# Re-ordering the state-space stage of a single-core decoder kernel: a chunk copy, two index computations, a lag table and the queue of projection units

## The reference, cut to what matters

```
z = h @ w_in            # q | 6 K/V tiles | branch gates | u (512 S5 channels) | merge gates
bu = einsum('gnc,btgc->btgn', b_bar, u)            # 32 groups, 64 complex states, 16 channels
h_t = a_bar * h_{t-1} + bu_t                       # scan over 512 tokens
y = Re(einsum('gcn,btgn->btgc', c, h)) + d * u     # then gelu, GLU, merge
```

## Time and profile before

| | |
|---|---|
| executions | 1350.45, 1352.05, 1352.19 us |
| the profiled execution | 1350.45 us, its span 1348.7 us |
| busy: PE, DVE, POOL, ACT | 1240.4, 832.8, 360.3, 306.0 us |
| mean granted PE clock | 0.967 of full |
| PE's share of the chain that ended last | 84% |

### The profile page before, as it was taken

One profiled execution on the slowest core, in us unless ns is written; L12 is line 12 of the kernel. 1 busy time (PEld: TensorE's weight loads), 2 busy tenths in 40 slices (PEclk: granted clock), 3 DMA queues, 4 the chain that ended last, 5 costly groups with the idle time before them and its releaser, 6 DMA issues.

```text
span 1348.7 us, 20585 instructions
## 1 busy us (share of the span) xinstructions
PE 1240.4 (92%) x7765; PEld 1007.8 (75%) x7765; DVE 832.8 (62%) x1370; ACT 306.0 (23%) x832; POOL 360.3 (27%) x422
## 2 busy tenths in 40 slices
PE   6889898999998679999999999977999999999995
PEld 5778776678886456555788888766888888888885
DVE  7997332237887468777755655657565464466445
ACT  3465111120010356556211001132000000000012
POOL 5953233322220013222111211110111112513441
PEclk9989998989999889999999999997999999999998
DMA  9324455567667224434653231420131131131101
GB/s 263 92 64 133 153 131 153 150 214 252 242 245 248 71 79 123 157 99 146 234 171 91 81 111 63 168 99 16 63 125 63 63 125 63 63 125 63 63 1 64
DMA packets 122002, 166.15 MB, mean 123 GB/s; under 512 B 36448, under 2 KB 90400, under 8 KB 117552
## 3 DMA queue, kind: packets, MB, share of 16 engines
q1 hardware_dynamic: 103408, 104.72, 25.0%
q0 software_dynamic: 8080, 50.58, 10.6%
q10 hardware_dynamic: 10416, 9.54, 2.2%
HBM read 159.34 MB, written 13.84 MB: 128 GB/s over the span
## 4 chain that ended last, share of the span: by engine, by line
PE 84%; DVE 9%; ACT 3%; issue 3%; POOL 0%; DMA 0%; another core or an unknown queue 0%; DVEq 0%; ACTq 0%; PEldq 0%
PE PS L2287 45%; PE PS L1874 14%; PE PS L2051 9%; PE PS L1851 4%; PE PS L2006 2%; PE PS L2195 2%; PE PS L2163 2%; DVE small L1663 2%; PE PS L2225 1%; DVE PS L1661 1%; DVE R L1681 1%; ACT QO L977 1%; PE PS L2030 1%; PE PS L1989 1%; DVE hT L1263 1%
## 5 line engine op out<-in xcount | busy, mean ns | idle before, releaser
L1874 PE MATMUL PS<-hT,stream 128*128 128x260 f32 (+1 forms) x800 | 186.0, 393 | 1.8 <-DVE hT L1263 0.7
L1874 PEld LDWEIGHTS PS<-hT,stream 128*128 128x128 f32 (+1 forms) x800 | 152.4, 193 | 33.4 <-issue 5.6
L2287 PE MATMUL PS<-R,stream 128*128 128x260 f32 x720 | 168.9, 383 | 2.4 <-PE PS L2287 2.4
L2287 PEld LDWEIGHTS PS<-R,stream 128*128 128x128 f32 x720 | 135.7, 190 | 25.8 <-issue 5.5
L2287 PE MATMUL PS<-R 128*128 128x260 f32 x576 | 134.4, 390 | 3.3 <-DVE R L1826 2.1
L2287 PEld LDWEIGHTS PS<-R 128*128 128x128 f32 x576 | 111.8, 194 | 22.1 <-DVE R L1826 2.5
L2051 PE MATMUL PS<-R 128*128 128x256 f32 (+1 forms) x544 | 121.2, 382 | 5.2 <-DVE R L1504 2.4
L2287 PE MATMUL PS<-R,QO 128*128 128x260 f32 x544 | 123.6, 383 | 1.4 <-DVE QO L1707 1.4
L1781 DVE TENSOR_TENSOR R<-PS,R 128x260 f32<-128x260 f32 x100 | 42.7, 427 | 129.6 <-PE PS L2287 128.9
L2051 PEld LDWEIGHTS PS<-R 128*128 128x128 f32 x544 | 101.4, 195 | 22.1 <-issue 6.1
L2287 PEld LDWEIGHTS PS<-R,QO 128*128 128x128 f32 x544 | 103.3, 190 | 17.6 <-DVE QO L1707 1.8
(11 more groups left out here) (421 smaller groups left out, 1929.2 us busy)
## 6 DMA issues: line engine op xcount, KB each, us to landing
stream<-in_cache_kv_slc SPq DMA_DIRECT2D x128, 128.0 KB, 2.1
stream<-in_w_mlp_up SPq DMA_DIRECT2D x8, 2048.0 KB, 8.3
stream<-in_w_mlp_down SPq DMA_DIRECT2D x8, 2048.0 KB, 7.7
stream<-in_w_in SPq DMA_DIRECT2D x4, 2048.0 KB, 9.4
stream<-in_state_kv_win SPq DMA_DIRECT2D x16, 512.0 KB, 5.6
stream<-in_w_in SPq DMA_DIRECT2D x8, 1024.0 KB, 7.8
out_kv_win_sample<-in_state_kv_win POOLq DMA_DIRECT2D x1, 8176.0 KB, 43.6
R<-in_cache_kv_slc SPq DMA_DIRECT2D x56, 128.0 KB
```

Source lines behind the costliest of these rows:

```text
L1874: ins = M(pair(u)[0:w, hf, 0:HALF], lhs[k], rhs[k][:, HALF * hf:HALF * hf + HALF], start=(k == 0), stop=(k == n - 1))
L2287: ins = M(product_of(w, i), lhs[:, k, :], rhs[:, k, :], start=(k == 0), stop=(k == nk - 1))
```

## The change

It does the following:

- the unit `kt` goes; `kk` makes the table in its final orientation, with `FP` as the stationary operand (128x128) and `C0P` as the moving one (32 columns), into full-width PSUM; `KPS` lives elsewhere;
- `u 3` stands ahead of the last two `ft` units, `y 0..3` one query tile later each (`y 3` behind `q 3`), and chunk ends 1 behind `q 4` where it was behind `q 7`;
- chunk copy 0 goes from ACT to DVE, ahead of the table; the page indices go ahead of the table too;
- chunk copy 1 stands behind the last `ft`, copies 2 and 3 behind `h0`, ahead of `toeplitz`;
- the S5 loop's fourth scratch buffer lies elsewhere, and DVE waits ahead of the loop for `toe_ready` and `gp_ready` (before, for `gp_ready` at ii == 1 and for no `toe_ready`).

```diff
-    head += [("ft", 0, q) for q in range(2)] + [("kt",)] + [("ft", 1, q) for q in range(2)] + u_tiles[3:]
+    head += [("ft", 0, q) for q in range(2)] + u_tiles[3:] + [("ft", 1, q) for q in range(2)]
-    rest = [q_units[6], ("h0",), q_units[7], q_units[4], ("y", 0), q_units[5], ("y", 1), q_units[0], ("y", 2),
-            q_units[1], ("y", 3), q_units[2], q_units[3], ("st",)]
+    rest = [q_units[6], ("h0",), q_units[7], q_units[4], q_units[5], ("y", 0), q_units[0], ("y", 1), q_units[1],
+            ("y", 2), q_units[2], q_units[3], ("y", 3), ("st",)]
-ENDS_BEHIND = [("h0",), ("q", 7), ("y", 0), ("y", 1)]
-COPIES_BEHIND = {("u", 3): 0, ("q", 6): 1, ("q", 7): 2, ("q", 4): 3}
+ENDS_BEHIND = [("h0",), ("q", 4), ("y", 0), ("y", 1)]
+COPIES_BEHIND = {("ft", 1, 1): (1,), ("h0",): (2, 3)}
-        KTS = QO[:, 6464:6976]
-        KPS = KVU[:, 1552:2064].rearrange("p (i c) -> p i c", i=NST)
+        KPS = QO[:, 6464:6976].rearrange("p (i c) -> p i c", i=NST)
-        W5 = [R[:, 14848:14848 + T]] + [QO[:, c:c + T] for c in (6464, 6976, 3 * NT)]
+        W5 = [R[:, 14848:14848 + T]] + [QO[:, c:c + T] for c in (6464, 6976, 7488)]
             elif k == 1:
                 eng.wait_ge(gp_ready, 1)
                 eng.wait_ge(pair_full, U_H0 + 1)
-                eng.wait_ge(toe_ready, 1)
...
-            dve.wait_ge(pair_free, U_KT + 1)
+            dve.wait_ge(pair_free, U_KK + 1)
             link(V.tensor_tensor(KPS[96:128], KPS[96:128], DI[96:128], ALU.add))
             dve.sem_inc(lag_ready, 1)
+            dve.wait_ge(pages_in, 16)
+            dve.wait_ge(masks_in, 16)
+            V.tensor_scalar(row_kv[:, :], pages[:, :], 2.0 * PAGE, consts[:, CO_ROW:CO_ROW + 1], ALU.mult, ALU.add)
...
+            V.tensor_scalar(row_cmp[:, :], pgr, 1.0, consts[:, CO_ROW + 1:CO_ROW + 2],
+                            ALU.mult, ALU.add).then_inc(rows_ready, 1)
+            dve.wait_ge(zero_ready, 3)
+            dve.wait_ge(pair_free, AT["u", 3] + 1)
+            for tau in range(TAU):
+                V.tensor_copy(UC[32 * tau:32 * tau + 32, 0::4, NB:NB + NK], uT[0:32, :, tau:T:TAU])
+            V.tensor_copy(UC[0:32, 0::4, 0:NB], uT[0:32, :, T:NT])
+            V.tensor_copy(UC[96:128, 0::4, NB + NK:UCW], uT[0:32, :, T:NT]).then_inc(chunk0_ready, 1)
             dve.wait_ge(pair_full, U_FT + 1)
             V.tensor_copy(TAB[:, 0, :, 0:64], BAS[:, 0])
...
             dve.wait_ge(pair_free, U_H0 + 1)
+            dve.wait_ge(toe_ready, 1)
+            dve.wait_ge(gp_ready, 1)
...
                 elif kind == "kk":
-                    for q in range(4):
+                    for i in range(NST):
                         for r in range(2):
-                            for i4 in range(4):
-                                i = 4 * q + i4
-                                ins = M(pr[32 * i4:32 * i4 + 32, 0, P * q:P * q + P], C0P[:, r, i, :], FP[:, r, i, :],
-                                        start=(r == 0), stop=(r == 1))
+                            ins = M(pr[:, 0, 32 * i:32 * i + 32], FP[:, r, i, :], C0P[:, r, i, :],
+                                    start=(r == 0), stop=(r == 1))
```

More of the change, by code:

```diff
@@ L302, in build @@
         chunks_ready = sem("chunks_ready")
+        chunk0_ready = sem("chunk0_ready")
         ends_full = sem("ends_full")
@@ L971, in chunk_copies @@
             def chunk_copies(ii):
-                act.wait_ge(pair_free, AT["u", 3] + 1)
+                act.wait_ge(pair_free, UNITS.index(("gemm", ("win", (C_U, 512)), 3, P, ("u", 3))) + 1)
                 act.wait_ge(zero_ready, 3)
@@ L1054, in _ @@
                 elif kind == "kk":
-                    ins = nc.scalar.activation(KTS, pr[:, 0, :], ACT.Copy)
-                elif kind == "kt":
                     ins = nc.scalar.activation(KPS, pr[:, 0, :].rearrange("p (i c) -> p i c", i=NST), ACT.Copy)
@@ L1083, in _ @@
                 ins.then_inc(pair_free, 1)
-                if label(unit) in COPIES_BEHIND:
-                    chunk_copies(COPIES_BEHIND[label(unit)])
+                for ii in COPIES_BEHIND.get(unit, ()):
+                    chunk_copies(ii)
                 if unit == ("h0",):
@@ L1367, in _ @@
                        (NST, m))
-            dve.wait_ge(pair_free, U_KT + 1)
+            dve.wait_ge(pair_free, U_KK + 1)
             link(V.tensor_tensor(KPS[96:128], KPS[96:128], DI[96:128], ALU.add))
             dve.sem_inc(lag_ready, 1)
+            dve.wait_ge(pages_in, 16)
+            dve.wait_ge(masks_in, 16)
+            V.tensor_scalar(row_kv[:, :], pages[:, :], 2.0 * PAGE, consts[:, CO_ROW:CO_ROW + 1], ALU.mult, ALU.add)
+            link(V.tensor_copy(pgf, pages[:, :]))
+            link(V.tensor_tensor(pgf.rearrange("p (x n) -> p x n", n=4), pgf.rearrange("p (x n) -> p x n", n=4),
+                                 consts[:, CO_PG:CO_PG + 4].unsqueeze(1).to_broadcast([P, 4 * NB, 4]), ALU.mult))
+            link(V.tensor_reduce(pgr, pgf.rearrange("p (x n) -> p x n", n=4), AX, ALU.add))
+            V.tensor_scalar(row_cmp[:, :], pgr, 1.0, consts[:, CO_ROW + 1:CO_ROW + 2],
[6 more added lines that the diff above has]
+            V.tensor_copy(UC[96:128, 0::4, NB + NK:UCW], uT[0:32, :, T:NT]).then_inc(chunk0_ready, 1)
             dve.wait_ge(pair_full, U_FT + 1)
@@ L1381, in _ @@
             dve.sem_inc(tables_done, 1)
[L1382 to L1390, removed]
             def sample_states():
-                w4 = [w[:, 0:P].rearrange("p (b i) -> p b i", b=NB) for w in W5[0:3] + [DEC]]
+                w4 = [w[:, 0:P].rearrange("p (b i) -> p b i", b=NB) for w in W5]
                 AR, AI, NI = (x.unsqueeze(1).to_broadcast([P, NB, NST]) for x in (abr, abi, nabi))
@@ L1984, in chunk_ends @@
                     pe.wait_ge(ends_free, ii)
-                pe.wait_ge(chunks_ready, ii + 1)
+                if ii == 0:
+                    pe.wait_ge(chunk0_ready, 1)
+                else:
+                    pe.wait_ge(chunks_ready, ii)
                 for r in range(2):
```

7 lines of the change are left out of this document (removed).

## The result

| | before | changed |
|---|---|---|
| median of 6 runs beside each other | 1352.8 us (1350.45 to 1355.72) | 1361.2 us (1356.15 to 1364.18) |
| ratio | | 1.006, 95% from 1.0036 to 1.0085 |
| profiled execution | 1350.45 us, span 1348.7 | 1360.14 us, span 1358.3 |
| granted clock, mean | 0.967 | 0.964 |

The change makes the kernel 8.4 us slower. Forecast were +5 and slower; 1361.2 lies inside the range (1352.8 to 1362.0) near its upper end, 4.2 us above the forecast of 1357. By the time alone it would fit the rival of the returning stand (1360.5) better; the traces have to decide. Later, on another chip where before takes 1327.6 us, the same change costs 1.0111 (1.0092 to 1.0129), 14.7 us.

The account below looks back on a forecast made before the run. PE was taken as the bound, standing still ahead of chunk ends 0 (for DVE's tables) and st; +5.1 (tables) and +0.2 (pauses) made +5.3, 1355.8 us profiled, 1357 typical, 8-in-10 range 1352.8 to 1362.

Parts of the forecast that it names:

- the rival of the returning stand: PE ahead of y 3: the 3.5 us wait for its own pair_full returns on top, 1360.5; 0.22 with like losses.
- The tables, on DVE: Index instructions (1.9) and copies (3.2) ahead of the tables delay them and chunk ends 0 by 5.1 us (3.9 to 7.1).
- kk and kt, on PE: kk takes 8.0 us instead of 1.95, kt's 0.9 goes; hidden by cover at u 3 and the tables, cost 0.
- theory A: Posed after the profile: the chain kk, ft, u 3 on PE sets when the tables come.
- B: The prediction's theory: the instructions added on DVE ahead of the tables delay them.
- The loop's new wait: DVE waits for ACT's toeplitz from 78.5 to 87.3; each y stands a tile later with 7.6 us over, cost 0.
- y 3 and the K/V tile: kv 0 0 waits for y 3's Gelus, some 4 us, against the lost 3.52 us stand ahead of st; +0.2 net.
- The odd stand: PE's 3.52 us idle ahead of st, waiting for its own pair_full, released by something the profile cannot name.
- Little remains: Rival: fast copies and a partly covered last Gelu, or tables and clock giving back, leave +2 to +2.7, 1354.3; 0.15.
- faster: Rival at the key scores: the shift breaks up pauses of 10 us together, giving 1347; 0.08.
- The tail by DVE's loop: Rival: DVE's loop is the limit, late toe_ready makes y 0 wait, 1361 or more; in the slower tail, no separate chance.

Follow-up runs that it names:

- the old order: The changed kernel with the order of q and y tiles as before, chunk ends 1 behind q 7; 1.011 (1.0074 to 1.0146) against before.
- the early copies: The kernel before with five small DVE instructions that begin BAS, two 128x16 copies among them, moved some 1.4 us earlier; 0.9952, 6.5 us faster.
- the fill: The kernel before with chunk ends 0 behind q 7, chunk ends 1 behind q 4, each y one tile later, y 3 still ahead of q 3; 0.9899, 13.6 us faster.
- one exchanged pair: The changed kernel with q 3 and y 3 exchanged, so that q 3 stands between y 3 and st; 1.0054 against before, 7.6 us faster than the changed kernel.

## Why the prediction was right, and where it was not

*The tables, on DVE (forecast +5.1 us, 3.9 to 7.1).* Right. Alone it measures +5.4 (3.5 to 7.4). In the trace chunk ends 0 go from 73.53 to 80.06: index instructions 1.8, four copies 3.5 (0.88 each, 0.7 was taken), two small ones 0.8 (0.4 was taken), and 0.3 that this execution was late from the start. The estimate by the fast form of the Trainium skill, "VectorE: DVE Perf Modes" (Mode 2×_2P, and the errata table), 0.33 us a copy and a shift of 3.6 us, is too low: beside a working POOL a copy took 0.88 to 1.03. That nothing is given back holds for this step alone (the tables take 13.6 us in both traces). In the whole change 2.2 to 3.2 us are: started at 69.9 to 71.4 us, the tables take 10.4 to 11.4, since POOL is done at about 75 and only their first part runs beside it.

*kk and kt, on PE (forecast 8.0 us, hidden, cost 0).* The price was off, and the cover was thinner than said. `kk` takes 8.3 to 10.9 us, because the clock falls in it (at full clock it would be some 7, less than the 8.0 taken), and `u 3` came so late that DVE stood still for it: 2.75 to 4.60 us where the small copy had been caught, 6.92 where not. That moves chunk ends 0 from 80.06 to 81.45 in the first kind of execution (1.4 us: 2.75 of waiting and 0.9 of slower copies, less 2.2 that the later tables give back) and from 74.98 to 81.94 in the second (7.0). As the first kind seems the common one (seven traces of eleven), the medians hardly show it: the change with and without the new `kk` is 1.0111 and 1.011, and `kk` alone is 1.0008. So cost 0 stands for the median, within some 5 us in the new order and 3 in the old, and failed for the profiled execution. The step of the forecast that was short is here: chunk ends 0 at 78.6, measured 81.45 to 81.94; of the first 2.9 us 1.5 are DVE's part and 1.4 `kk`'s.

*The comparison of the two profiled executions* hides this: before was caught by the memset (5.8 us) and the changed one was not, and both had other luck as well: the two `u` tiles ahead of `kk` took 14.3 us in one and 16.0 in the other, 1.7 us that also appear in some traces with the packed `kk`. Read alone, the pair says that `kk` and not DVE's new work delays the tables (theory A). The medians say B.

*The loop's new wait (cost 0).* Right, and for the reason given: `toeplitz` ended 6 us later than forecast (93.3), and still no `y` waited. With the old order 4.11 us of it show.

*y 3 and the K/V tile (forecast +0.2 net).* The mechanism was right to 0.4 us: a wait of 4.12, ended by L1061. But it was set against the stand of 3.52 us ahead of `st` as if that belonged to the kernel. It comes with the chip: every one of the six traces of the 1352 chips has late updates of this kind, the seven of the 1327 chip have none, three of them with `st` right behind `q 3` as before. Where such an update falls, and whether PE stands still for it, changes with the order: ahead of `st` in before and with the early copies, ahead of `q 2` in the fill; in the changed kernel PE does not stand for one before the key scores. And a slow tile follows the wait (15.98 against 14.22 us), which before had behind its own stand only in part (15.14). So this step costs 1.4 on a 1352 chip (4.12 + 0.82 - 3.52) and on the 1327 chip 5.9 by the trace (4.13 + 1.76), 8.8 (5.8 to 11.8) by the median. With 6.5 and 1.4 for the tables, by the traces, the sum is 13.8 there, 14.7 measured; less the stand (3.5) and the tiles that were half slow before already (0.9) it is 9.4 on a 1352 chip, 8.4 measured. Single terms are known to 2 or 3 us only (by its median the 6.5 is 5.4), so that the sums come so close is in part luck.

*The number.* The forecast of 1357 held the tables at 78.6 where they came 3 us later, and a step for `y 3` of 0.2 where it costs 1.4; together with 0.8 that the median of before rose in the six runs beside the changed kernel this is a little more than the 4.2 us missed by. The forecast's own range, 1354.8 to 1359.5, does not come out of the bounds that it names: 3.9 to 7.1 in place of 5.1 give 1355.8 to 1359.0.

*The rivals.* The odd stand did not return, though the time came out where that rival had put it. Little remains and faster fell: the pauses in the key scores are still there after (215 to 221 and 252 to 257 us) and shifted along, as the argument against them said. They too come with the chip: the rows of the key scores have 5.2 to 6.2 us of idle time between them in the six traces of the 1352 chips, and none in the seven of the 1327 chip. The tail by DVE's loop did not come either.

## What to carry to other kernels

Price an edit by the engine that stands idle behind it: with one more tile put in front of chunk ends 0 the tables came just as late, but PE no longer stood still for them, and the first K/V tile started 8.4 us earlier. When a unit is moved next to one that shares its buffers, count what stands between its slow evacuation and the next user; one exchanged pair was worth 7.6 us. And compare medians with single traces before believing either: an instruction of 0.18 us that is sometimes caught for 3.59 can make the trace of a pair tell the wrong cause, and a stretch of low clock far behind the edit (3.5 us here) can pass for a gain.

## What the hardware showed beside this

*Late updates.* On the 1352 chips a wait for PE's products sometimes ends 3 to 5 us behind the recorded end of the last product, as in the three rows below, and whoever waits stands still; I read it as an update of a semaphore that arrives late. ACT in the kernel before, the changed one and the filled one:

```profile
148.11 0.60 ACT L1012 ACTIVATE QO<-PS 128x520 f32<-128x520 f32 x1 [9.62 <-remote]
```
```profile
170.31 0.60 ACT L1010 ACTIVATE QO<-PS 128x520 f32<-128x520 f32 x1 [12.18 <-remote]
```
```profile
121.18 0.60 ACT L1012 ACTIVATE QO<-PS 128x520 f32<-128x520 f32 x1 [8.98 <-remote]
```

The products waited for ended at 144.87, at some 166.4 and at 116.4 us. Three or four such places are in each trace of the 1352 chips between 100 and 260 us, none in those of the 1327 chip. Nothing here shows what causes them; key pages are being transferred at those times. On the 1327 chip the key scores last 102 us from the first to the last, in every trace, on the 1352 chips 117 to 119; that is 15 or 16 of the 25 us between the chips.

*The clock inside a busy stretch.* 64 small products with 128x128 weights took 8.27, 8.48, 8.67, 10.47, 10.67 and 10.94 us in six traces, with no idle time ahead of them. The granted clock explains the spread: it was 0.87 over the 8.27 us, 0.82 over the 8.67, 0.66 over the 10.67 and 0.64 over the 10.94, and time multiplied by clock gives 7.0 to 7.2 us in all four, an estimate of what `kk` takes at full clock. In five of the six the 16 transposes behind it took 3.16 to 3.65 us as well, in all seven traces with the packed `kk` 1.97.
